# A streaming encoder step: the attention's probabilities divided on ScalarE, each denominator taken before the next maxima

## The reference, cut to what matters

```
def sink_softmax(s, sink):
    m = jnp.maximum(jnp.max(s, axis=-1, keepdims=True), sink)
    e = jnp.exp(s - m)
    return e / (jnp.sum(e, axis=-1, keepdims=True) + jnp.exp(sink - m))
```

## Time and profile before

| | |
|---|---|
| median of three runs | 1792.86 us (1791.85 to 1793.93) |
| the profiled execution's own time | 1792.29 us |
| its span, first to last instruction | 1790.5 us |
| TensorE busy | 1765.8 us (99%) |
| VectorE busy | 781.5 us (44%) |
| ScalarE busy | 505.2 us (28%) |
| GpSimd busy | 529.1 us (30%) |

### The profile page before, as it was taken

The page is one execution under the profiler, slowest core; times in us unless marked ns, Lnnn a source line. Parts: engine busy times, 40 slices in busy tenths (PEclk is TensorE's granted clock), DMA queues, the critical chain, the costliest instruction groups (busy, mean ns, idle before and its releaser), DMA issues.

```text
span 1790.5 us, 29954 instructions
## 1 busy us (share of the span) xinstructions
PE 1765.8 (99%) x10741; PEld 1639.3 (92%) x10741; DVE 781.5 (44%) x1641; ACT 505.2 (28%) x1155; POOL 529.1 (30%) x486
## 2 busy tenths in 40 slices
PE   6999999999999999999999999999999999999999
PEld 5999999989999999999999999999999888888887
DVE  7754540554545421111556566552322453453433
ACT  6311110134333310000344434330011443343332
POOL 4356420322232242332655555552433000000000
PEclk8999999999999999999999999999999999999999
DMA  7432211343444332212333432334534675664654
GB/s 257 141 92 66 86 48 52 91 113 95 111 109 126 93 96 71 77 55 75 98 99 90 121 101 85 99 120 150 155 118 139 200 243 164 211 222 165 199 165 136
DMA packets 246128, 220.81 MB, mean 123 GB/s; under 512 B 26018, under 2 KB 210676, under 8 KB 244596
## 3 DMA queue, kind: packets, MB, share of 16 engines
q1 hardware_dynamic: 171828, 176.68, 31.4%
q10 hardware_dynamic: 74232, 43.23, 8.8%
HBM read 169.71 MB, written 52.24 MB: 124 GB/s over the span
## 4 chain that ended last, share of the span: by engine, by line
PE 96%; DVE 1%; DMA 1%; ACT 1%; ACTq 0%; issue 0%; POOL 0%; SPq 0%; DVEq 0%; POOLq 0%
PE p L1835 20%; PE p L1837 19%; PE p L1836 19%; PE p L1926 7%; PE p L1928 7%; PE p L1930 7%; PE p L901 2%; PE p L592 1%; PE p L1870 1%; PE p L1869 1%; PE p L1871 1%; PE p L620 1%; PE p L604 1%; PE p L913 1%; PE p L919 1%; PE p L912 1%
## 5 line engine op out<-in xcount | busy, mean ns | idle before, releaser
L1835 PE MATMUL p<-x_hi,w_lo 128*128 128x384 f32 x2016 | 697.6, 346 | 0.0
L1837 PE MATMUL p<-x_hi,w_hi 128*128 128x384 f32 x2016 | 675.3, 335 | 0.0
L1836 PE MATMUL p<-x_lo,w_hi 128*128 128x384 f32 x2016 | 674.3, 334 | 0.0
L1835 PEld LDWEIGHTS p<-x_hi,w_lo 128*128 128x128 f32 x2016 | 378.8, 188 | 15.6 <-issue 13.5
L548 POOL TENSOR_TENSOR w_hi<-raw,small 128x512 fp32r<-128x512 f32 x164 | 173.5, 1058 | 726.8 <-PE p L1837 710.8
L1836 PEld LDWEIGHTS p<-x_lo,w_hi 128*128 128x128 f32 x2016 | 379.1, 188 | 0.2
L1837 PEld LDWEIGHTS p<-x_hi,w_hi 128*128 128x128 f32 x2016 | 378.3, 188 | 0.0
L2137 DVE TENSOR_TENSOR w_lo<-raw,w_hi 128x512 fp32r<-128x512 f32 x192 | 132.1, 691 | 206.9 <-ACT w_hi L1783 206.9
L552 POOL TENSOR_TENSOR w_lo<-raw,w_hi 128x512 fp32r<-128x512 f32 x164 | 216.2, 1318 | 12.8
L1783 ACT ACTIVATE w_hi<-raw 128x512 fp32r<-128x512 f32 x192 | 120.8, 631 | 242.6 <-PE p L1930 213.1
L1926 PE MATMUL p<-w_hi,x_lo 128*128 128x512 f32 x570 | 160.2, 389 | 0.0
(11 more groups left out here) (191 smaller groups left out, 1784.1 us busy)
## 6 DMA issues: line engine op xcount, KB each, us to landing
raw<-in_w_out SPq DMA_DIRECT2D x192, 256.0 KB, 3.5
raw<-in_w_in SPq DMA_DIRECT2D x164, 256.0 KB, 4.3
h_t<-xn SPq DMA_DIRECT2D x126, 192.0 KB, 1.9
work<-h_t SPq DMA_DIRECT2D x24, 384.0 KB, 6.1
out<-work SPq DMA_DIRECT2D x36, 256.0 KB, 4.6
work<-h_t ACTq DMA_DIRECT2D x16, 512.0 KB, 4.6
work<-h_t ACTq DMA_DIRECT2D x32, 256.0 KB, 4.2
work<-in_x_prompt SPq DMA_DIRECT2D x32, 256.0 KB, 4.9
```

The lines of the kernel that those rows point to most:

```text
L1835: pe.matmul(out, w_lo[:, k, :], x_hi[:, k, tok], start=(k == 0), stop=False)
L1836: pe.matmul(out, w_hi[:, k, :], x_lo[:, k, tok], start=False, stop=False)
L1837: mm = pe.matmul(out, w_hi[:, k, :], x_hi[:, k, tok], start=False, stop=(k == KT - 1))
```

## The change

The four multiplications a group leave VectorE's `divide`, which keeps the denominator and its reciprocal. ScalarE gets a `divide` that waits for the reciprocal and does the same multiplications as copies with a scale a row. On ScalarE it stands behind the exponentials of its group; so in part 0 the order is exponentials 0, division 0, exponentials 1, division 1, then the bank copies; in part 1 the division of group 2 stands ahead of the outputs' copy, and that of group 3 ahead of the next tile's loads. On VectorE the denominator of group 0 moves ahead of the maxima of group 1.

```
--- before
+++ after
             def divide(self, t, g):            # class attend_act
+                act = self.act
+                i = g % 2
+                act.wait_ge(sa_den, 8 * t + (2 * g + 2))
+                for r in range(GQA):
+                    act.wait_ge(sa_e, 20 * t + (5 * g + r + 2))
+                    act.activation(a_p[i][:, r, :], a_p[i][:, r, :], ACT.Copy, scale=a_den[i][:, r:r + 1])\
+                       .then_inc(sa_p, 1)
...
                 def part_0():
                     self.exps(t, 0)
+                    self.divide(t, 0)
                     self.exps(t, 1)
+                    self.divide(t, 1)
                     self.copy_probs(t, 0)
                     self.copy_probs(t, 1)
 
                 def part_1():
                     self.exps(t, 2)
+                    self.divide(t, 2)
                     self.copy_out(t, 0)
...
                         self.copy_probs(t, 2)
                         self.exps(t, 3)
+                    self.divide(t, 3)
                     if not (type(t) is int and t == NTP - 1):
                         self.load(t + 1)
...
                 dve.wait_ge(sa_den, 8 * t + (2 * g + 2))      # class attend_dve, divide
-                for r in range(GQA):
-                    dve.tensor_scalar(a_p[i][:, r, :], a_p[i][:, r, :], a_den[i][:, r:r + 1], None, ALU.mult)\
-                       .then_inc(sa_p, 1)
...
                 def part_0():                                 # class attend_dve, tile
                     self.shift(t, 0)
+                    self.divide(t, 0)
                     self.shift(t, 1)
-                    self.divide(t, 0)
                     self.divide(t, 1)
```

More of the change, by code:

```diff
@@ L671, in exps, with divide @@
                                    accum_out=a_sum[i][:, r:r + 1]).then_inc(sa_e, 1)
+            def divide(self, t, g):
+                act = self.act
+                i = g % 2
+                act.wait_ge(sa_den, 8 * t + (2 * g + 2))
+                for r in range(GQA):
+                    act.wait_ge(sa_e, 20 * t + (5 * g + r + 2))
+                    act.activation(a_p[i][:, r, :], a_p[i][:, r, :], ACT.Copy, scale=a_den[i][:, r:r + 1])\
+                       .then_inc(sa_p, 1)
             def copy_probs(self, t, g, heads=range(2)):
```

## The result

The changed kernel takes 1835.59 us (median; 1835.31 to 1836.46) against 1792.44 beside it: a ratio of 1.0237, with a 95% interval of 1.0225 to 1.0249. It is slower by 43 us. The prediction had the sign and both waits, but 1823.0 us, and the time lies 3.6 us above the range. In the profiled execution (1835.33 us) the span is 1833.5 us against 1790.5.

A forecast was written before the change was run, and what follows sets the result against it. TensorE was taken to bound the kernel, with 96% of the chain of waits. Tile 0's 2.3, 6 x (2.05 + 2.35) and tile 7's 2.05 make 30.75 us: 1792.29 + 30.75 = 1823.0 us, range 1812 to 1832.

The forecast's parts named there:

- both waits: TensorE waits for ScalarE's bank copy at two turns, 13 or 14 times of about 2 us, 28 to 31 us.
- The steps on the order of work: Denominator of group 0 ahead of group 1's maxima: maxima 0.54 us late, group 1's exponentials too, TensorE doesn't notice.
- allowed 0.1 for such things: Group 1's division on ScalarE: 0.1 us for added waits and their register arithmetic, within the 2.05 us of lateness.
- first hold: Turn 0,1, tiles 1 to 7: group 1's four scaled copies delay the bank copy; 2.05 us each, bounds 1.5 and 2.6.
- second hold: Turn 3,1, tiles 1 to 6: group 3's division delays load issues, then the bank copy; 2.35 us each, bounds 1.5 and 3.4.
- Tile 0's wait on the division: VectorE's divisions beside GpSimd's work held a TensorE turn in tile 0 for 1.58 us; that goes.
- 1.85 and 0.15: Tile 0: second turn of group 3 net 1.85 us late; 0.15 left of the first turns' 2.05 us lateness.
- The extra 0.3 for loads that land late: End of tile 0: last load, issued at 391.85, lands at 396.15 or later, delaying tile 1's scores by 0.3 us.
- the last sentence of the sum: Whole kernel: no loss of clock on top, as the granted clock stood at 1.00 through tile 0's 1.6 us idle.
- The rival that the first or the second hold alone would appear: Attention tiles: only one of two turns waits; first alone 1805.8 us, chance 0.05; second alone 1808.7 us, chance 0.03.
- not slower: Turn copies: ScalarE reaches them within 0.2 us of room, only tile 0 gains; 1790.6 us, chance 0.02.
- more than forecast: A third hold or late loads in each tile: up to 1.2 us for each of seven, 1831 us, chance 0.08.

The follow-up runs named there:

- second hold alone: Kernel before, with the next tile's query and key loads waiting on ScalarE for group 3's denominator, VectorE still dividing: 1812.17 us, ratio 1.0099.
- second hold filled: Changed kernel with 14 matmuls that nobody reads ahead of waiting turn 3,1 in tiles 0 to 6: 1833.47 us, ratio 1.0226.
- both filled: Changed kernel with unread matmuls, 14 ahead of turn 0,1 (tiles 1 to 7), 18 ahead of turn 3,1 (tiles 0 to 6): 1823.96 us, ratio 1.0169.
- run without holds: Changed kernel with loads spread and group 0's bank copies ahead of group 1's division: 1791.86 us, ratio 0.9991; repeated with more rounds, 1791.61 us, 0.9988.

## Why the prediction was wrong

The steps on the order of work were right. VectorE's maxima of group 1 begin 0.61 us after the start of the sum for the denominator of group 0, where 0.41 was taken (tile 3 of the kernel after; 0.23 of it is idle behind the reciprocal, where the waits of `shift` stand):

```profile
487.18 0.16 DVE L771 TENSOR_TENSOR small<-small 128x4 f32<-128x4 f32 x1 [2.03 <-ACT work L670]
487.38 0.18 DVE L773 RECIPROCAL small<-small 128x4 f32<-128x4 f32 x1
487.79 0.42 DVE L758 CUSTOM_DVE_ANT_0 work<-p,work,sink_row 128x192 f32<-128x192 f32 x1 [0.23 <-DVE small L773]
```

The sum had allowed 0.1 for such things. The first hold was put at 2.05 us and measured 2.08. The second was put at 2.35 and measured 2.47; the 0.4 taken from denominator to first issue, for which no row was given, was 0.58 (468.59 to 469.17), and the train took the 4.89 that were forecast. Tile 7 has the first hold alone, as forecast. Tile 0's wait on the division went, and its second turn of group 3 came 1.85 us late, counted from the tile's first scores, where 1.85 and 0.15 were forecast. The extra 0.3 for loads that land late can't be seen in the changed kernel, but only because the clock had fallen there: the outputs ahead of the scores took 2.7 us (394.73 to 397.47) where they took 1.5 before (392.55 to 394.06):

```profile
394.73 1.97 PE L620 MATMUL p<-work 128*64 128x128 f32 x16
...
397.47 0.82 PE L592 MATMUL p<-work 64*64 64x192 f32 x16
```

In the three runs with the same late train and no fall at this place TensorE stands idle ahead of these scores for 0.59, 0.47 and 0.28 us (second hold alone, second hold filled, both filled).

The scaled copy has 444 ns on average, against 442 of the exponential that it was compared with:

```profile
L679 ACT ACTIVATE work<-work,small 128x192 f32<-128x192 f32 x128 | 47.8, 444 | 16.5 <-DVE small L773 16.5
```

Four take 1.49 us, so one follows the other after (1.49 - 0.44) / 3 = 0.35, the 1.4 for four that was taken. The Trainium skill's "ScalarE: Activation LUTs", section "What ACT_TABLE_LOAD costs", gives an estimated 186 + 93 + 0.833 x 192 = 439 ns for one and 346 from one to the next; the trace agrees.

The step that failed is the last sentence of the sum: "I expect no loss of clock on top: through the 1.6 us of idle in tile 0 the granted clock stood at 1.00". The row was read rightly, and it bore less than was put on it. It ends at 390.00, and the idle stretch at 389.94; a fall, where there is one in the kernel after, begins 0.4 to 1.3 us behind the hold. The next window of the kernel before shows that none came:

```profile
390.00:394.00 4.00, 3.95 (x47) 3.25 (x51) 1.71 (x4) 0.98 (x2) 1.25 (x1) 1.00 0.67 115
```

But one idle stretch without a fall doesn't show that such stretches have none: of the seven first holds of the changed kernel, all 1.9 us long, one had a fall behind it, and with the second hold taken away four of the same seven had. The changed kernel has 14 longer stretches than that one, and eight falls, 13.6 us that the sum lacked: 30.75 + 13.6 = 44.4, where 43.15 were measured (part of the difference is tile 0, where the slow stretch covers the wait for the loads). Neither the bounds nor the rivals held this term, which is why the range ended too low; the rival "more than forecast" came closest, with up to 8.4 us where 12.4 were missing, but for another reason.

The rival that the first or the second hold alone would appear is refuted: fifteen waits. The rival "not slower" named the right point, whether ScalarE is back at the copies in time. The run without holds shows that with the order mended and the loads spread the divisions on ScalarE cost nothing that can be measured; in the order of the change ScalarE comes two microseconds late.

Open is which holds have a fall behind them. The runs show a fall behind three of seven second holds, four of seven first holds, eight of fourteen of both kinds, and six of seven first holds where the second was filled. Their idle times don't settle it. Of the 27 holds with 1.86 to 2.01 us of idle in these four runs 14 had a fall behind them, and like ones went either way; the seven of 2.28 to 2.78 us, the second holds of the changed kernel, all had one. Whether their length is the reason isn't shown, since all seven stand at one place of the tile in one kernel. The four idle stretches of 1.1 to 1.6 us in tile 0 (one of the kernel before, two of the run with the second hold alone, one of that with the second hold filled) had none. It wasn't tried how short a hold must be in the other tiles to have none.

## What to carry to other kernels

Work moved to an engine with idle time is paid for by what stands behind it in that engine's order, here a copy that frees a bank and a train of DMA issues, and not by its own duration: the same divisions cost 43 us in one order, and nothing that can be measured in another with the loads spread. Where TensorE was never idle, a new idle stretch of two microseconds may cost nearly as much again through its clock (1.7 us here), and one quiet stretch in the old trace is no proof against it: the range has to reach that far. A filled hold is a quick test for it: it tells the clock's share of a wait from the wait itself.

## What the runs showed of the hardware

Some 29 us of matmuls that nobody reads (7 x 1.83 and 7 x 2.31) took 11.6 us off the changed kernel (1835.59 to 1823.96), by keeping TensorE's clock at 2.4 GHz through its waits. And the falls are not tied to one hold: with one of the two filled they went to the other, six of them where there had been one.
